# Expert weights of a two-layer decoder trunk: the ring of 2 MB buffers filled, waited for and freed in halves of 1 MB

## The reference, cut to what matters

```python
def expert_block(args):                      # xb: the tokens of one expert
    xb, e = args
    return (jax.nn.silu(xb @ w_gate[e]) * (xb @ w_up[e])) @ w_down[e]
...
    gate = p_g * v2 / jnp.sum(v2, axis=-1, keepdims=True)
    eid = (g_sel * EXPERTS_PER_GROUP + e_sel).reshape(-1).astype(jnp.int32)
    y = grouped_swiglu(xt, eid, w_gate, w_up, w_down).reshape(N, TOP_K_IN_GROUP, D)
    out = jnp.sum(y * gate[..., None].astype(y.dtype), axis=1)
```

## Time and profile before

| | us |
|---|---|
| median of 3 runs | 1498.46 (1496.92 to 1500.74) |
| the profiled execution, its own time | 1493.24 |
| its span | 1491.4 |
| TensorE busy in the span | 1385.7 (93%) |
| VectorE busy | 590.6 (40%) |
| ScalarE busy | 326.6 (22%) |

### The profile page before, as it was taken

How to read it: one execution, slowest core, us unless ns; L and a number is a source line. 1 busy time by engine, 2 the same in 40 slices (tenths; PEclk the granted TensorE clock), 3 DMA queues, 4 the chain that set the end, 5 groups by cost and what they waited for, 6 DMA issues and landing times.

```text
span 1491.4 us, 16620 instructions
## 1 busy us (share of the span) xinstructions
PE 1385.7 (93%) x6272; PEld 618.7 (41%) x6337; DVE 590.6 (40%) x1084; ACT 326.6 (22%) x632; POOL 103.0 (7%) x199
## 2 busy tenths in 40 slices
PE   7989998999999999999899978976999999999987
PEld 3445456333333334333454555442333333333333
DVE  5555124133333334233649774132334334332334
ACT  4445111101101101111337664110111111110110
POOL 1001000200000000000000132003000000000000
PEclk9999999999999999999999999987999999999999
DMA  9105365999999999999800020737999999999994
GB/s 315 68 0 198 129 263 203 357 428 426 428 426 425 427 428 428 427 427 419 296 0 1 25 93 1 309 152 275 425 428 427 426 427 426 427 427 427 429 426 203
DMA packets 57332, 457.53 MB, mean 307 GB/s; under 512 B 15516, under 2 KB 22220, under 8 KB 32312
## 3 DMA queue, kind: packets, MB, share of 16 engines
q1 hardware_dynamic: 50928, 447.96, 72.8%
q0 software_dynamic: 5504, 8.68, 1.6%
q10 hardware_dynamic: 840, 0.06, 0.0%
HBM read 459.50 MB, written 10.53 MB: 315 GB/s over the span
## 4 chain that ended last, share of the span: by engine, by line
PE 63%; DMA 23%; DVE 8%; ACT 3%; issue 1%; POOL 0%; SPq 0%; ACTq 0%; DVEq 0%; POOLq 0%
PE ps L1480 20%; PE ps L1155 19%; DMA arena<-in_moe_w_up 14%; PE ps L1494 10%; DMA arena<-in_moe_w_gate 9%; PE ps L1502 6%; PE ps L1473 1%; DVE mix L1774 1%; ACT arena L999 1%; DVE small L1773 1%; DVE arena L1850 1%; DMA mix<-scratch_xn,whole 1%; PE ps L1486 1%; DVE xT L1629 1%; DMA gains<-in_norm_ffn 1%
## 5 line engine op out<-in xcount | busy, mean ns | idle before, releaser
L1480 PE MATMUL ps<-arena,xT 128*64 128x512 f32 x2048 | 461.9, 605 | 26.0 <-DMA arena<-in_moe_w_gate 20.5
L1480 PEld LDWEIGHTS ps<-arena,xT 128*64 128x64 f32 x2048 | 151.6, 139 | 319.2 <-issue 319.2
L2086 DVE TENSOR_TENSOR x<-ps,x 128x1024 f32<-128x1024 f32 x120 | 146.5, 1225 | 219.0 <-PE ps L1502 216.7
L1494 PE MATMUL ps<-arena,xT 128*64 128x512 f32 x1024 | 226.8, 595 | 0.0
L1155 PE MATMUL ps<-xT,arena 128*128 128x512 f32 x384 | 170.6, 599 | 1.8 <-DVE xT L1629 1.4
L1502 PE MATMUL ps<-mix,xT 128*128 128x512 bf16 x660 | 157.4, 379 | 6.4 <-issue 4.8
L1494 PEld LDWEIGHTS ps<-arena,xT 128*64 128x64 f32 x1024 | 70.7, 137 | 131.8 <-issue 127.9
L1155 PE MATMUL ps<-arena,mix 128*128 128x512 f32 (+1 forms) x288 | 119.4, 570 | 0.0
L1502 PEld LDWEIGHTS ps<-mix,xT 128*128 128x128 bf16 x720 | 65.5, 98 | 119.5 <-issue 48.7
L1155 PEld LDWEIGHTS ps<-xT,arena 128*128 128x128 f32 x384 | 72.6, 192 | 92.5 <-issue 89.6
L2069 DVE SCALAR_TENSOR_TENSOR xT<-ps,cur,xT 128x512 f32<-128x512 f32 x32 | 24.0, 751 | 207.3 <-PE ps L1480 207.3
(11 more groups left out here) (268 smaller groups left out, 1110.8 us busy)
## 6 DMA issues: line engine op xcount, KB each, us to landing
arena<-in_moe_w_gate SPq DMA_DIRECT2D x64, 2048.0 KB, 32.3
arena<-in_moe_w_up SPq DMA_DIRECT2D x64, 2048.0 KB, 32.0
arena<-in_moe_w_down SPq DMA_DIRECT2D x64, 2048.0 KB, 34.9
arena<-in_w_out SPq DMA_DIRECT2D x2, 4096.0 KB, 13.5
arena<-in_dsa_w_in SPq DMA_DIRECT2D x1, 5120.0 KB, 16.1
arena<-in_w_mem_kv SPq DMA_DIRECT2D x2, 2048.0 KB, 9.0
scratch_xn<-arena SPq DMA_DIRECT2D x8, 512.0 KB, 2.9
scratch_rep<-scratch_bias SPq DMA_DIRECT2D x1, 3840.0 KB, 17.9
```

The costliest lines, as they stand in the source:

```text
L1480: ins = pe.matmul(ps[e * CAP:(e + 1) * CAP, bank, :], tokT[:, k, e * CAP:(e + 1) * CAP], rows_in[u][:, k, :], start=k == 0, stop=k == KD - 1)
L1494: ins = pe.matmul(ps[e * CAP:(e + 1) * CAP, BANK_Y + c, :], hT[:, j, e * CAP:(e + 1) * CAP], rows_down[u][:, j, c * 512:(c + 1) * 512], st ...
L2086: dve.tensor_tensor(x[:, t, :], ps[:, b:b + 2, :].rearrange("p a n -> p (a n)"), x[:, t, :], ALU.add).then_inc(s_, 1)
```

## The change

Each 2 MB unit becomes two slots of 1 MB (`NS` = 20), with the same total memory. A gate or up matrix is loaded as two halves of the contraction (`k` 0 to 3 and 4 to 7, for each partition 8 KB in one piece). A down matrix is loaded as two halves of its columns (for each partition 4 rows of 2 KB that lie 4 KB apart). Each half has its own `dma_start`, so a pair has 12 loads in place of 6. TensorE waits for the two experts' halves in front of the 16 matmuls that use them, and signals after each 16 matmuls (`gate_half`, `gate_psum`, `up_half`, `up_psum`; `y_psum` was counted for each column half already). Slot i of pair p is (12p + i) mod 20, and waits for the product half that used it before. The overflow loads (`weights`) stay whole. Three semaphores are merged into others (`broute` into `onehot`, `restored` into `stored`), so that the semaphores suffice.

```diff
+        half_at = [PHYS[q // 2] * UNIT + (q % 2) * (UNIT // 2) for q in range(NS)]
+        half_in = [area(at, KD // 2, FE) for at in half_at]
+        half_down = [area(at, KF, D // 2) for at in half_at]
...
-            def pair_weights(L, j, u, p, n, first=False):
+            def half_weights(L, i, q, p, n, first=False):
 
                 if not first:
-                    if j in (0, 1):
+                    if i in (0, 1):
+                        sp.wait_ge(up_half, n + (-1))
+                    elif i in (2, 3):
                         sp.wait_ge(m["up_psum"], n + (-1))
-                    elif j in (2, 3):
+                    elif i in (4, 5):
+                        sp.wait_ge(m["y_psum"], n * 2 + (-3))
+                    elif i in (6, 7):
                         sp.wait_ge(m["y_psum"], n * 2 + (-2))
+                    elif i in (8, 9):
+                        sp.wait_ge(gate_half, n)
                     else:
                         sp.wait_ge(m["gate_psum"], n)
-                weights(L, p * 2 + j % 2, j // 2, u, landed[u])
+                e, kind, h = p * 2 + i % 2, i // 4, i // 2 % 2
+                if kind < 2:
+                    src = a["moe_w_gate" if kind == 0 else "moe_w_up"]
+                    src = src[L, bass.ds(e, 1)].rearrange("a (p k) n -> p (a k) n", k=KD)[:, h * KD // 2:(h + 1) * KD // 2, :]
+                    sp.dma_start(half_in[q], src).then_inc(landed[q // 2], 16)
+                else:
+                    src = a["moe_w_down"][L, bass.ds(e, 1)].rearrange("a (p j) n -> p (a j) n", j=KF)[:, :, h * D // 2:(h + 1) * D // 2]
+                    sp.dma_start(half_down[q], src).then_inc(landed[q // 2], 16)
...
                 wait_filled(sp, f"{L}.out.{NT - 1}.1")
-                for j in range(2):
-                    pair_weights(L, j, 6 + j, 1, NP * L + 1, True)
+                for i in range(4):
+                    half_weights(L, i, 12 + i, 1, NP * L + 1, True)
                 sp.wait_ge(xn_stored, 16 * NT * (L + 1))
-                pair_weights(L, 5, 5, 0, NP * L, True)
+                for i in (10, 11):
+                    half_weights(L, i, i, 0, NP * L, True)
...
-                        sp.dma_start(b_route[:, :, c0:c1], a[name].unsqueeze(0).to_broadcast([P, 2, c1 - c0])).then_inc(ld["broute"], 16)
+                        sp.dma_start(b_route[:, :, c0:c1], a[name].unsqueeze(0).to_broadcast([P, 2, c1 - c0])).then_inc(ld["onehot"], 16)
...
-                            pe.wait_ge(ld["onehot"], 32)
+                            pe.wait_ge(ld["onehot"], 64)
...
+                def both_halves(bank, halves, times, half_done, s_):
+
+                    for h in range(2):
+                        pe.wait_ge(landed[halves[2 * h] // 2], times[h] * 32)
+                        for k in range(KD // 2):
+                            for e in range(2):
+                                ins = pe.matmul(ps[e * CAP:(e + 1) * CAP, bank, :], tokT[:, h * KD // 2 + k, e * CAP:(e + 1) * CAP],
+                                                half_in[halves[2 * h + e]][:, k, :], start=h + k == 0, stop=h * KD // 2 + k == KD - 1)
+                        ins.then_inc((half_done, s_)[h], 1)
+
+                def down_halves(halves, times, s_):
+
+                    for c in range(2):
+                        pe.wait_ge(landed[halves[2 * c] // 2], times[c] * 32)
+                        for j in range(KF):
+                            for e in range(2):
+                                ins = pe.matmul(ps[e * CAP:(e + 1) * CAP, BANK_Y + c, :], hT[:, j, e * CAP:(e + 1) * CAP],
+                                                half_down[halves[2 * c + e]][:, j, :], start=j == 0, stop=j == KF - 1)
+                        ins.then_inc(s_, 1)
...
-                    for j in (0, 1):
-                        pe.wait_ge(landed[units[j]], times[j] * 16)
                     pe.wait_ge(m["xt_sbuf"], n * 2 + (2 * L + 2))
-                    both(BANK_GATE, units[0:2], m["gate_psum"])
+                    both_halves(BANK_GATE, units[0:4], times[0:2], gate_half, m["gate_psum"])
```

More of the change, by code:

```diff
@@ L61 @@
 NU = 10
+NS = 2 * NU
 R = NG + NE
@@ L406, in hybrid_trunk @@
         i8 = route_area[:, 1248:1280].bitcast(U32).rearrange("p (t n) -> p t n", t=NT)
-        ld = {n: sem(f"ld_{n}") for n in ["mem", "x0", "x1", "x2", "x3", "win0", "win1", "prm", "onehot", "gains", "broute", "wkv", "win", "winq", "wing", "wv", "wg",
+        ld = {n: sem(f"ld_{n}") for n in ["mem", "x0", "x1", "x2", "x3", "win0", "win1", "prm", "onehot", "gains", "wkv", "win", "winq", "wing", "wv", "wg",
                                           "wout", "wr", "bias", "wuv", "ovl"]}
@@ L451, in hybrid_trunk @@
         bias_stored, bias_spread = sem("bias_stored"), sem("bias_spread")
-        landed = [sem(f"landed{u}") for u in range(NU)]
+        landed = [sem(f"landed{v}") for v in range(NU)]
+        gate_half, up_half = sem("gate_half"), sem("up_half")
         gathered = sem("gathered")
@@ L462, in hybrid_trunk @@
         ov_added = [sem(f"ov_added{L}") for L in range(2)]
-        stored, restored = sem("stored"), sem("restored")
+        stored = sem("stored")
         def wait_alone(eng, s, value):
@@ L614, in _ @@
                 wait_filled(sp, f"{L}.out.0.0")
-                for j in range(5):
-                    pair_weights(L, j, j, 0, NP * L, True)
+                for i in range(10):
+                    half_weights(L, i, i, 0, NP * L, True)
                 for t in range(NT):
@@ L620, in _ @@
                 wait_filled(sp, f"{L}.out.{NT - 1}.1")
-                for j in range(2):
-                    pair_weights(L, j, 6 + j, 1, NP * L + 1, True)
+                for i in range(4):
+                    half_weights(L, i, 12 + i, 1, NP * L + 1, True)
                 sp.wait_ge(xn_stored, 16 * NT * (L + 1))
-                pair_weights(L, 5, 5, 0, NP * L, True)
+                for i in (10, 11):
+                    half_weights(L, i, i, 0, NP * L, True)
                 if L == 0:
                     wait_filled(sp, "1.memV.1")
[L627 to L630, removed]
+                for i in range(4, 8):
+                    half_weights(L, i, 12 + i, 1, NP * L + 1, True)
+                for i in range(8, 12):
+                    half_weights(L, i, (12 + i) % NS, 1, NP * L + 1)
                 sp.wait_ge(chosen, 2 * L + 2)
                 sp.dma_start(scratch_ov.ap()[L], ov_code[0:OVMAX, :]).then_inc(ov_stored, 16)
-                with sp.Fori(0, (NP - 6) // 5) as i:
+                with sp.Fori(0, (NP - 6) // 5) as v:
                     for r in range(2, 7):
-                        for j in range(6):
-                            pair_weights(L, j, (6 * r + j) % NU, i * 5 + r, i * 5 + (NP * L + r))
+                        for i in range(12):
+                            half_weights(L, i, (12 * r + i) % NS, v * 5 + r, v * 5 + (NP * L + r))
                 for p in range(NP - 4, NP):
-                    for j in range(6):
-                        pair_weights(L, j, (6 * p + j) % NU, p, NP * L + p)
+                    for i in range(12):
+                        half_weights(L, i, (12 * p + i) % NS, p, NP * L + p)
                 sp.wait_ge(ov_stored, 16 * (L + 1))
@@ L673, in _ @@
                         for t in range(NT):
-                            sp.dma_start(out[0, t * P:(t + 1) * P, :], x[:, t, :]).then_inc(restored, 16)
-                        sp.wait_ge(restored, 16 * NT)
+                            sp.dma_start(out[0, t * P:(t + 1) * P, :], x[:, t, :]).then_inc(stored, 16)
+                        sp.wait_ge(stored, 2 * 16 * NT)
             sp.wait_ge(scattered, 16 * 2 * NT * 2)
@@ L1517, in pair @@
                 def pair(n, units, times, first=False, second=False):
-                    for j in (0, 1):
-                        pe.wait_ge(landed[units[j]], times[j] * 16)
                     pe.wait_ge(m["xt_sbuf"], n * 2 + (2 * L + 2))
-                    both(BANK_GATE, units[0:2], m["gate_psum"])
+                    both_halves(BANK_GATE, units[0:4], times[0:2], gate_half, m["gate_psum"])
                     if not first:
                         combine_of(n + (-1), (0, 1), not second)
-                    for j in (2, 3):
-                        pe.wait_ge(landed[units[j]], times[j] * 16)
-                    both(BANK_UP, units[2:4], m["up_psum"])
+                    both_halves(BANK_UP, units[4:8], times[2:4], up_half, m["up_psum"])
                     if not first:
@@ L1535, in pair @@
                     tokens_T(m["xt_psum"])
-                    for j in (4, 5):
-                        pe.wait_ge(landed[units[j]], times[j] * 16)
                     pe.wait_ge(m["ht_sbuf"], n + 1)
-                    down(units[4:6], m["y_psum"])
+                    down_halves(units[8:12], times[4:6], m["y_psum"])
                 n0 = NP * L
                 def ring(p):
-                    return [(6 * p + j) % NU for j in range(6)]
```

(3 more changed lines are left out.)

## The result

The changed kernel takes 1520.21 us (median of 4 runs, 1519.03 to 1521.04), the kernel before, beside it on the same chip, 1498.24. The ratio is 1.0144, with a 95% interval of 1.0126 to 1.0162: slower by about 22 us. The forecast had slower, by 10.5 us.

What follows compares the result with a forecast made beforehand. The weight loads, not TensorE, were taken to set the pace. -8 - 6 - 1 + 22 + 3 = +10 us on the profiled 1493.2 gave 1503.5, a median of about 1509 us; range 1484 to 1522.

Steps and rivals of the forecast that it cites:

- the stream's term: Expert weight loads behind each stream's start: shorter pieces lower the rate, +22 us (0 to 26).
- I take 403, nearest the row of the same length: Down loads in 2 KB pieces: 403 GB/s, chosen near the 399 measured for position biases in 2 KB pieces.
- the line through the 4 KB row: Output weights in 4 KB pieces ran at 421 GB/s: 3.0 ns per piece, so 2 KB pieces at 413.
- The rule of 3 cycles: Fixed overhead of about 3 cycles per DMA piece: 2 KB at 411 GB/s, 15 us in all, sum about 0.
- completions, +3: 174 more transfers behind the streams' starts, each with its own completion: +3 us (0 to 11).
- The edges, -15: Stage ends and starts shortened by finer waits: -8 us at the ends, -6 at layer 1's start, -1 at layer 0's.
- the -1: Layer 0's start: down loads enter a queue still holding the ups; earlier halves save 1 us (0 to 3).
- No cost for pieces: Rival: engines keep 427 GB/s at 2 and 8 KB, only the edges move, -15 us, 1483.5; chance 0.24.
- half the cost: Rival: 2 KB pieces run at 413 GB/s, no change of time, 1496 to 1500; chance 0.16.
- Every 1 MB transfer pays its own completion: Rival: 0.06 us for each transfer in full, pieces as at 399 GB/s, +25 us, 1523; chance 0.06.
- transfers in series: Rival: weight transfers run one behind the other, 1 MB at 341 GB/s, 37 us a pair; chance 0.01.
- At nothing: SP: SP's 12 load issues of about 0.4 us take 5 of a pair's 30 us, so cost nothing.

Runs made afterwards that it cites:

- the experiment that has nothing else: The kernel before, whole transfers and waits, with only the down matrices written in 2 KB pieces: 1523.04 against 1497.10 us, ratio 1.0169.
- the version with 8 KB pieces: The changed kernel with down matrices halved by rows, not columns, so all pieces have 8 KB: 1495.27 us against 1496.62 for the kernel before, 0.9986.
- End only: The kernel before with halves only in each layer's last pair, all else in whole transfers: ratio 0.9994 to the kernel before.
- the edges-only kernel: The kernel before with halves only in each layer's last pair and pair 1's down matrices: 1489.87 against 1496.52 us, 0.9953; repeated, 0.9953.
- the three kernels with 8 KB pieces alone: The kernel before with 8 KB pieces in whole transfers (1.0075) or halves (1.0054); the changed kernel with down matrices halved by rows (0.9986).

## Why the prediction was right and wrong

**Right: what sets the time.** The loads set the pace, the edges can be shortened and the shorter pieces cost more than that. The rate fell in both phases, to 407 to 409. That is below the 410 at which I had said that the forecast would be wrong. TensorE's waits for gate weights start earlier in layer 0, as expected (the product after the first wait starts at 488 us, where it was 512; the second fence is the kernel before):

```profile
488.49 3.65 PE L1525 MATMUL ps<-arena,xT 128*64 128x512 f32 x16 [1.48 <-DMA arena<-in_moe_w_gate]
493.37 3.65 PE L1525 MATMUL ps<-arena,xT 128*64 128x512 f32 x16 [1.23 <-DMA arena<-in_moe_w_gate]
```
```profile
512.28 7.09 PE L1480 MATMUL ps<-arena,xT 128*64 128x512 f32 x32 [1.68 <-DMA arena<-in_moe_w_gate]
```

**Wrong: the size of the stream's term.** The mechanism was right and one term of the sum was mis-sized. The step that failed is "I take 403, nearest the row of the same length" with the 5.2 ns per piece drawn from it, and the 423.5 for 8 KB that followed. Measured: 420 GB/s for 8 KB and 386 for 2 KB. An engine moves 16 KB in 613.9 ns at 427, 623 at 420.5 (the mean of 420 and 421) and 679 at 386. That is 9.5 ns for one piece more and 65 for seven more, so a piece costs 9.3 ns, not 5.2, and not the 3.0 of the line through the 4 KB row. By the same figure the 4 KB row itself would be at 409, and it stood at 421: other loads of the same trace, in windows of a few us with their own mix behind them, were no good price list. Why they ran faster stays open. The rule of 3 cycles (Trainium skill, "DMA: Bandwidth & Descriptors", "Why small descriptors are slow (HBM only)") had the sign right; the 411 GB/s estimated from it for 2 KB (410, if its 67 and 515 are worked out) is not what this trace shows, 386.

In microseconds: the down matrices' pieces cost 25 in the experiment that has nothing else (forecast 18). For gate and up I take two thirds, their share of the bytes, of the 8 to 11 us that 8 KB pieces cost in all: 5 to 7 (forecast 5). On the medians the stream's term is 30 to 32, where I had 22.

**Wrong: completions, +3.** Whole transfers gave 1.0075 and halves 1.0054 with the same pieces, so the term is 0 within the noise. It was meant as a hedge, and covered part of the miss by luck.

**The edges, -15.** Read from the trace, they came nearly as forecast: the down product ends about 5 us after the last landing (forecast 4 to 5), and from layer 1's first weight load to the issue of pair 1's down matrices it is 93.5 us in place of 99.6, -6.1 (forecast -6; 4.0 of it from half of the gate product and 1.9 from the indirect load of the token rows, 8.67 in place of 10.59 us). In layer 0's start nothing is seen of the -1. By the difference of kernels with the same 8 KB pieces the finer waits are worth 10 to 13 us, 2 to 5 less than the forecast's 15. Each of these differences has an interval of about 3 us to either side, and the version with 8 KB pieces has no column halves at the end, so it stays open whether the forecast had too much.

**The sum closes.** On the medians, 25 + 5 to 7 - 10 to 13 gives +17 to +22; measured +22, the upper end. The traces give the same sum with larger terms. A down pair of 4.19 MB at 386 takes 10.87 us in place of 9.82, and gate and up at 420.5 take 19.95 in place of 19.65: 30 x 1.04 + 28.5 x 0.30 = 40 us, where I had 22. Less 6.1 at layer 1's start and about 4 at each end (layer 0's taken as layer 1's) that is +26, and the span grew by 26.7. The difference between the two sums is mostly that of the baseline: the profiled execution of before lay 5.2 us under its median. What made it the faster one is not shown.

**The rivals.** "No cost for pieces" and "half the cost" fall with the windows at 420 and 386. "Every 1 MB transfer pays its own completion" named nearly the right time (1523) with the wrong mechanism: equal rates with 1 and 2 MB transfers rule it out, and the same rows rule out transfers in series. (Its sum takes the edges at -12, where the forecast has -15; with -15 it names about 1520.)

**At nothing: SP.** I had 12 issues of 0.4 us. In fact SP is held while it issues into a full queue:

```profile
444.62 2.49 SPq L563 DMA_DIRECT2D arena<-in_moe_w_up  x4
447.20 23.72 SPq L566 DMA_DIRECT2D arena<-in_moe_w_down  x4
471.13 4.89 SPq L563 DMA_DIRECT2D arena<-in_moe_w_gate  x4
```

Four down halves take 23.7 us to issue, and with the others SP is busy for the whole pair (31.1 us); the chain of waits even puts 30% of the span on it. One could suspect that this issuing sets the rate. It does not: the engines never ran dry (share 1.03), and gate, down and up halves land 14.4, 20.5 and 21.2 us (medians of the profile page) after their issue, so there was always work in the queue. Nor is it the number of loads: with six loads a pair and 2 KB pieces in the down matrices alone SP is held as long (20 to 25 us for two of them). In whole transfers of 8 KB pieces it is held nearly all the time from 500 us on, at 421 GB/s. The chain names the place where the work stands in line, not what makes it slow.

## What to carry to other kernels

In a kernel whose time is a stream of loads, a finer wait is worth what it takes off the two ends of the stream, once per stage, while a shorter piece is paid for in every byte between them. Halve along the dimension that keeps pieces long, or halve only where a stage starts and ends: here the latter turned +22 us into -7, and the former into -2. And take the price of a piece length from a small experiment on the stream itself, in place of a window over some other load.

## What the runs showed of the hardware

- Each piece cost about 9.3 ns of one DMA engine's time (an estimate from the three rates): 16 KB (427 GB/s), 8 KB (420), 2 KB (386). It made no difference that shows whether the transfer was 1 or 2 MB, or which side was cut: with runs of 16 KB in DRAM and 2 KB pieces in the buffer, the down matrices alone brought the mean of the three kinds to 412 or 413, which makes about 386 for them (16 engines move 3 x 262144 bytes at 412.5 GB/s in 1906.5 ns; less 2 x 613.9 that leaves 679 ns for an engine's 16 KB).
- A pause of about 2 us on TensorE was sometimes followed by a lower granted clock, sometimes not. End only, after 2.02 us of wait, the granted clock was 0.53 and then 0.62, so first near the lower of its levels of 1.2 and 2.4 GHz, and the product took 8.78 us:

```profile
668.00:670.00 2.00, 0.15 (x2) 0.18 (x4) 1.39 (x3) 1.63 (x3) 0.00 (x0) 1.00 1.02 426
670.00:672.00 2.00, 2.00 (x6) 0.64 (x6) 0.67 (x2) 0.00 (x0) 0.00 (x0) 0.53 1.01 422
672.00:674.00 2.00, 2.00 (x8) 0.77 (x6) 0.00 (x0) 0.00 (x0) 0.00 (x0) 0.62 1.00 420
```

  In the repeat of the edges-only kernel the product after 2.18 us of wait ran at 1.00 and took 7.09:

```profile
1422.58 7.09 PE L1507 MATMUL ps<-arena,xT 128*64 128x512 f32 x32 [2.18 <-issue]
```
```profile
1422.00:1424.00 2.00, 1.42 (x8) 0.68 (x10) 1.14 (x3) 0.44 (x1) 0.00 (x0) 1.00 0.98 410
```

  So 1.7 us a time hang on something that I can't foresee from the length of the wait. A part of the spread between single executions may come from it; that was not tested.
- The indirect load of the token rows at layer 1's start took 10.59 us beside 16 KB pieces, 8.67 in the changed kernel, 8.51 to 8.79 in the three kernels with 8 KB pieces alone, and 6.86 where all pieces had 2 KB. So this short load of another queue landed sooner when the pieces of the stream were short.
